# A two-block transformer kernel: another order of the new projection, the memory's norm inside the last pair of experts, and the router's token lists made first

## What is computed

```python
def moe_swiglu(h, router_w, wg, wu, wd):
    ...
    logits = (t @ router_w).astype(jnp.float32)
    top_logits, top_idx = lax.top_k(logits, TOP_K)
    top_w = jax.nn.softmax(top_logits, axis=-1)
    ...
    for e in range(N_EXPERTS):
        y = y + gates[:, e:e + 1] * swiglu(t, wg[e], wu[e], wd[e])
...
        x = x + gate2 * y
    return rmsnorm(x, final_norm_w)
...
        h = rms_norm(x, g_mix[layer])
        proj = h @ w_in[layer]
...
        log_f = jax.nn.log_sigmoid(f_logit.astype(jnp.float32)
...
        mkv = rms_norm(mem, g_mem[layer]) @ w_mem_kv[layer]
```

## Time and profile before

| | |
|---|---|
| median of 3 runs | 1531.88 us (1529.24 to 1533.62) |
| the profiled execution | 1529.77 us, span 1528.0 us |
| PE busy | 1458.8 us, 95% of the span |
| DVE busy | 1135.8 us, 74% |
| ACT busy | 769.4 us, 50% |
| experts | 610.3 to 1030 us |
| weights of the new projection first used | 1075.27 us |

### The profile page before, as it was taken

One profiled execution on the slowest core, in us unless ns is written; L12 is line 12 of the kernel. 1 busy time (PEld: TensorE's weight loads), 2 busy tenths in 40 slices (PEclk: granted clock), 3 DMA queues, 4 the chain that ended last, 5 costly groups with the idle time before them and its releaser, 6 DMA issues. The chain is left out here.

```text
span 1528.0 us, 20898 instructions
## 1 busy us (share of the span) xinstructions
PE 1458.8 (95%) x8225; PEld 1261.3 (83%) x8225; DVE 1135.8 (74%) x1245; ACT 769.4 (50%) x806; POOL 4.1 (0%) x7
## 2 busy tenths in 40 slices
PE   3998999999999997999999999999999999999999
PEld 3876799899798886878887888787787778799997
DVE  6888687876778764888988888988787677555544
ACT  1534333333463553767677677764566443443332
POOL 0000000000000000000000000000000000000000
PEclk9999999999999996999999999999999999999999
DMA  9776378877665470899998998982544335445652
GB/s 322 252 295 228 119 251 281 300 260 247 205 223 166 167 240 22 289 327 319 349 335 296 350 336 304 343 296 84 172 161 167 133 112 165 138 153 169 210 164 103
DMA packets 198424, 345.72 MB, mean 226 GB/s; under 512 B 11633, under 2 KB 90065, under 8 KB 193233
## 3 DMA queue, kind: packets, MB, share of 16 engines
q1 hardware_dynamic: 190592, 339.76, 64.5%
q10 hardware_dynamic: 7760, 4.97, 1.1%
HBM read 343.65 MB, written 1.05 MB: 226 GB/s over the span
## 5 line engine op out<-in xcount | busy, mean ns | idle before, releaser
L2000 DVE TENSOR_TENSOR wlo<-raw,whi 128x2048 fp32r<-128x2048 f32 (+2 forms) x220 | 480.0, 2192 | 163.2 <-ACT whi L637 159.4
L637 ACT ACTIVATE whi<-raw 128x2048 fp32r<-128x2048 f32 (+2 forms) x220 | 403.5, 1837 | 360.2 <-PE ps L1256 243.0
L1254 PE MATMUL ps<-whi,AH 128*128 128x512 f32 (+1 forms) x816 | 321.6, 394 | 9.0 <-DVE wlo L2000 6.0
L1256 PE MATMUL ps<-whi,AL 128*128 128x512 f32 (+1 forms) x816 | 312.2, 383 | 0.0
L1255 PE MATMUL ps<-wlo,AH 128*128 128x512 f32 (+1 forms) x816 | 312.0, 382 | 0.0
L1254 PE MATMUL ps<-AH,whi 128*128 128x256 f32 x896 | 256.3, 286 | 2.2 <-DVEq L2100 1.5
L1255 PE MATMUL ps<-AL,whi 128*128 128x256 f32 x896 | 254.8, 284 | 0.0
L1256 PE MATMUL ps<-AH,wlo 128*128 128x256 f32 x896 | 254.7, 284 | 0.0
L1254 PEld LDWEIGHTS ps<-whi,AH 128*128 128x128 f32 x816 | 153.8, 188 | 48.2 <-DVE wlo L2000 15.6
L1256 PEld LDWEIGHTS ps<-whi,AL 128*128 128x128 f32 x816 | 153.5, 188 | 28.1
L1254 PEld LDWEIGHTS ps<-AH,whi 128*128 128x128 f32 x896 | 173.3, 193 | 3.6 <-DVEq L2100 1.8
...
## 6 DMA issues: line engine op xcount, KB each, us to landing
...
```

Of the source, the lines that this page charges most:

```text
L637: act.activation(whi[:, h, 0:n], raw_at[s][:, 0:n], ACT.Copy).then_inc(w_hi, 1)
L1254: pe.matmul(o, sh, mh, start=first, stop=False)
L1256: return pe.matmul(o, sl, mh, start=False, stop=last)
L2000: dve.tensor_tensor(wlo[:, h, 0:n], raw_at[s][:, 0:n], whi[:, h, 0:n].bitcast(fp), ALU.subtract)\
```

## The change

Five things are changed:

1. A Sqrt on an idle column stands ahead of `first_squares`, so ACT loads that table there.
2. In the router DVE writes the sum of the two choices to `lg2` directly behind the choice; the constants of the lists are made earlier and the gates after the first selection. 20 fillers stand ahead of the transposes (15 before), and 4 new ones behind the token matmuls.
3. The loop over pairs has three passes, and the fourth is written out. In it ACT's queue loads the memory into `TS`, ACT squares it at j = 5 and 6, DVE makes the norm at j = 8, 11, 12 and 13 of the first expert; the two gathers are replaced by transposes of the memory (`memory_transposes`), whose features take the place of the next pair's. The gate of `Y`'s first half moves into the pass.
4. Behind the experts the memory's units follow directly. `X` is completed and normed in halves, with the final norm's scale and weight in one operation. The transposes of the new input stand inside and behind the fourth unit, followed by 3 fillers. ACT copies out the memory's products, which DVE did before.
5. The forget gate's matmul uses split operands (`three`), 24 matmuls.

```diff
-            for k0 in (0, 4):
-                m_unit(w, w_mkv, k0, 4, 0)
-            sp.wait_ge(*w.free_at[N_RAW])
-            sp.dma_start(memx, t["mem_2"][0].rearrange("(i p) n -> p i n", p=128)).then_inc(mem_in, 16)
-            for k0 in (0, 4):
-                m_unit(w, w_mkv, k0, 4, 512)
+            m_matrix(w, w_mkv, 0, 2)
...
             def first_squares(n):
 
+                act.activation(idle_col, idle_col, ACT.Sqrt)
                 act.wait_ge(x_part, 3 * n + 1)
...
+            def memory_load():
+                act.dma_start(TS[:, :, :], t["mem_2"][0].rearrange("(i p) n -> p i n", p=128)).then_inc(mem_in, 16)
+            def memory_norm(j):
+                if j in (5, 6):
+                    act.wait_ge(mem_in, 16)
+                    act.activation(flatA[:, 1024 * (j - 5):1024 * (j - 4)], TS[:, j - 5, :], ACT.Square,
+                                   accum_out=ss[:, j - 5:j - 4]).then_inc(sq_done, 1)
+                if j == 9:
+                    root(2)
+            def memory_high(bank, q):
...
+                    ins = act.activation(AH[:, kk, :], ps[:, bank + k // 2, SEQ * (k % 2):SEQ * (k % 2) + SEQ], ACT.Identity,
+                                         scale=vec[:, V_GMEM + kk:V_GMEM + kk + 1])
+                ins.then_inc(e_high, 1)
...
                         if j == 18:
+                            if last and x:
+                                next_input(1)
                             output(x, 1)
-                next_input(1)
+                if not last:
+                    next_input(1)
...
-            act.wait_ge(mem_in, 16)
-            squares(memx)
-            features_high(vec[:, V_GMEM:V_GMEM + 8])
-            his(w, 2)
-            act.wait_ge(a_ready, 2 * 6)
-            act.wait_ge(x_ready, 1)
-            squares(X)
-            act.wait_ge(x_ready, 2)
-            squares(X)
-            his(w, 2)
-            second_half(vec[:, V_GMIX:V_GMIX + 8])
+            first_unit = w.unit - LEAD
+            def memory_out(c):
+                act.wait_ge(w_used, first_unit + 2 * c + 2)
+                bank = 2 * ((PAIR_MOE + c) % 4)
+                link(act.activation(mkv[:, c], ps[:, bank:bank + 2, :], ACT.Copy))
+                act.sem_inc(ps_free, 1)
+            def half_squares(c, n):
+                for i in range(TT):
+                    act.wait_ge(x_ready, n + i * c)
+                    act.activation(flatA[:, 1024 * c + 512 * i:1024 * c + 512 * i + 512], X[:, i, 512 * c:512 * c + 512],
+                                   ACT.Square, accum_out=ss[:, 2 * c + i:2 * c + i + 1]).then_inc(sq_done, 1)
+                if c:
+                    root(2)
+            hi(w)
+            half_squares(0, 1)
+            hi(w)
+            half_squares(1, 2)
+            hi(w)
+            memory_out(0)
+            half_squares(0, 4)
+            half_squares(1, 5)
+            hi(w)
+            features_high(vec[:, V_GMIX:V_GMIX + 8], (0,))
+            memory_out(1)
+            features_high(vec[:, V_GMIX:V_GMIX + 8], (1,))
...
+            def memory_transposes(q, bank):
+                pe.wait_ge(ts_ready, 2 * stage[0] + 1 + q)
+                for k in range(4):
+                    for i in range(TT):
+                        ins = pe.transpose(ps[:, bank + k // 2, SEQ * (k % 2) + 128 * i:SEQ * (k % 2) + 128 * (i + 1)],
+                                           TS[:, i, 512 * q + 128 * k:512 * q + 128 * (k + 1)], ident)
+                ins.then_inc(e_gather, 1)
...
-                gather(w, TT, (1,))
+                if not last:
+                    gather(w, TT, (1,))
                 put_back(pair(w), 1, 1)
+                if last:
+                    pe.sem_inc(ps_free, N_EXPERTS * E_PAIRS - N_EXPERTS // 2 * E_PAIRS_2)
+                    pe.wait_ge(e_in, 2 * e + 4)
...
-            transposes(w, 15)
+            transposes(w, 20)
...
...
-                ins = pe.matmul(ps[:, bank, 16:24], ones[:, 0:128], oh[:, 0, i, :], start=i == 0, stop=i == TT - 1)
+                ins = pe.matmul(ps[:, bank, 16:24], ones[:, 0:128], lg2[:, i, :], start=i == 0, stop=i == TT - 1)
             ins.then_inc(small_mm, 1)
+            keep_busy(w, 4)
             pe.wait_ge(crowd_set, 1)
             crowd = pe.value_load(crowded[0:1, 0:1], min_val=0, max_val=1)
...
-            transposes(w, 8)
-            keep_busy(w, 4)
-            new_input()
-            m_matrix(w, 2)
-            stage[0] += 1
-            transposes(w)
-            keep_busy(w, 11)
+            stage[0] += 2
+            m_matrix(w, 1)
+            bank = pair(w)
+            m_unit(w, bank, 0, 4, KT)
+            def mixed_transposes(q):
+                pe.wait_ge(ts_ready, 2 * stage[0] - 1 + q)
+                bank = pair(w)
...
+                ins.then_inc(tp_done, 1)
+            m_unit(w, bank, 4, 4, KT, between=lambda: mixed_transposes(0))
+            mixed_transposes(1)
+            keep_busy(w, 3)
...
+                    pe.wait_ge(fox_w_set, 1)
                     for k in range(KT):
-                        ins = pe.matmul(ps[0:40, bank, 0:SEQ], wsm[:, k, 48:88], AF[:, k, :], start=k == 0, stop=k == KT - 1)
+                        ins = three(ps[0:40, bank, 0:SEQ], fox_w_high[:, k, :], fox_w_low[:, k, :], AH[:, k, :], AL[:, k, :],
+                                    k == 0, k == KT - 1)
                     ins.then_inc(small_mm, 1)
...
+            dve.tensor_scalar(upto, cst[:, C_CAUSALT:C_CAUSALT + 128], 0.0, None, ALU.is_equal)
+            dve.tensor_tensor_scan(numbers, ones[:, :], ones[:, :], 0.0, ALU.mult, ALU.add)
+            dve.memset(slot_of, 0.0)
...
+            both(dve.tensor_tensor(lg2, oh[:, 0], oh[:, 1], ALU.add), tokens_set, 1)
             dve.tensor_tensor(mm2[:, 2, :], mm2[:, 1, :], mm2[:, 0, :], ALU.subtract).then_inc(g_vec, 1)
             for i in range(TT):
                 dve.wait_ge(t_split, i + 1)
...
                 free(w, dve.tensor_tensor(t_low[:, i, :].rearrange("p (b n) -> p b n", b=2), ps[:, bank:bank + 2, :],
                                           t_high[:, i, :].bitcast(fp).rearrange("p (b n) -> p b n", b=2), ALU.subtract))
-            dve.wait_ge(g_act, 3)
-            link(dve.tensor_scalar(mm2[:, 4, :], mm2[:, 3, :], 1.0, None, ALU.add))
-            link(dve.reciprocal(mm2[:, 5, :], mm2[:, 4, :]))
...
-            dve.tensor_tensor(gates[:, :, 0:8], lgt, lg2, ALU.add)
-            dve.tensor_scalar(upto, cst[:, C_CAUSALT:C_CAUSALT + 128], 0.0, None, ALU.is_equal)
-            dve.tensor_tensor_scan(numbers, ones[:, :], ones[:, :], 0.0, ALU.mult, ALU.add)
-            dve.memset(slot_of, 0.0)
-            both(dve.tensor_tensor(oh[:, 0], oh[:, 0], oh[:, 1], ALU.add), tokens_set, 1)
             dve.wait_ge(small_mm, 3)
             bank = bank_of(w)
-            dve.tensor_tensor(slot_of[:, :, 0:8], ps[:, bank, 0:16].rearrange("p (i e) -> p i e", i=TT), oh[:, 0], ALU.mult)
+            dve.tensor_tensor(slot_of[:, :, 0:8], ps[:, bank, 0:16].rearrange("p (i e) -> p i e", i=TT), lg2, ALU.mult)
...
+            def memory_norm(j):
+                m, y, s = ms[:, 0:2], rs[:, 0:2], nt[:, 0:2]
+                if j == 8:
+                    counts["sq"] += 2
+                    dve.wait_ge(sq_done, counts["sq"])
+                    link(dve.tensor_scalar(m, ss[:, 0:2], 1.0 / D, EPS, ALU.mult, ALU.add))
+                    dve.reciprocal(y, m).then_inc(root_in, 1)
+                    counts["root"] += 1
+                if j == 11:
+                    dve.wait_ge(root_out, counts["root"])
+                    link(dve.tensor_tensor(s, y, y, ALU.mult))
+                    link(dve.tensor_tensor(s, s, m, ALU.mult))
+                    link(dve.tensor_scalar(s, s, -0.5, 1.5, ALU.mult, ALU.add))
+                    link(dve.tensor_tensor(y, y, s, ALU.mult))
+                if j in (12, 13):
+                    q = j - 12
+                    cut = slice(512 * q, 512 * q + 512)
+                    for i in range(TT):
+                        ins = dve.tensor_scalar(TS[:, i, cut], TS[:, i, cut], rs[:, i:i + 1], None, ALU.mult)
+                    ins.then_inc(ts_ready, 1)
+                    counts["ts"] += 1
+            def memory_low(bank, q):
...
+                    ins = dve.scalar_tensor_tensor(AL[:, kk, :], ps[:, bank + k // 2, SEQ * (k % 2):SEQ * (k % 2) + SEQ],
+                                                   vec[:, V_GMEM + kk:V_GMEM + kk + 1], AH[:, kk, :].bitcast(fp),
+                                                   ALU.mult, ALU.subtract)
+                ins.then_inc(e_in, 1)
+            def gated(c):
+                cut = slice(512 * c, 512 * c + 512)
+                rows_ = GB[:, 1, cut].rearrange("p (o n) -> p o n", o=1).to_broadcast([128, TT, 512])
+                link(dve.tensor_tensor(Y[:, :, cut], Y[:, :, cut], rows_, ALU.mult))
...
+                        if last and x and j == 19:
+                            gated(0)
+                            add_back(1, 1)
```

(46 more changed lines are left out.)

181 lines of the change are left out of this document (123 added, 58 removed).

## The result

| | before | changed |
|---|---|---|
| median | 1530.56 us (1525.43 to 1533.62, 4 runs) | 1506.37 us (1505.7 to 1507.2, 4 runs) |
| ratio | | 0.9838, 95% interval 0.9817 to 0.9859 |
| profiled execution | 1529.77 us, span 1528.0 us | 1505.82 us, span 1504.0 us |
| PE busy | 95% of the span | 96% |

The forecast was 1506.0. The next table puts PE's start at one place after the other beside each other. The last column says what the stretch ahead of the place gained in these two executions.

A forecast was written before the change was run, and what follows sets the result against it. PE was taken as the bound, so only its waits, fillers and half-clock time pay. 1.7 + 7.5 - 2.3 + 18.1 + 0.8 = 25.8 us, giving 1506 us against the median 1531.88; range 1499 to 1516.

The forecast's parts named there:

- Part 1: At the norms, the Sqrt table load moved ahead of the squares shortens PE's waits: gain 1.7 us, bounds 0.4 and 3.4.
- gain 1.3: At the second norm (402.94), PE's 2.02 us wait shrinks by the table load's time, 1.3 us.
- Part 2: Router: earlier token lists start the gather 5.9 us earlier, the clock gives 1.6 more: gain 7.5 us, bounds 5.0 and 11.5.
- clock term: Router's gather: only about 1 us runs at half clock, so it takes 4.3 us instead of 5.88.
- Part 3: Last pair of experts: DVE's inserted norm steps delay PE 2.6 us; cheaper transposes return 0.3: net cost 2.3 us.
- (c): Clock returns no sooner in the router and falls again ahead of the last put-back: 1509 to 1510 us, 12%.
- Part 4: Last put-back to new projection: waits, fillers and transposes fall away, start at 1057.1 instead of 1075.27: gain 18.1 us.
- The forget matmul: Forget gate: the 40-row matmul (3.65 us) becomes 24 matmuls of 256 columns, 2.9 us: gain 0.8 us.
- (a): DVE becomes the bound in the last pair and the projection behind it: 1512 to 1516 us, 15%.
- (b): The clock holds through the router: 4 us more gained, 1502 us, 12%.
- (d): Norm is ready early but PE waits for `e_in` behind DVE's queue, half the gap stays: 1515 to 1520 us, 4%.
- (e): Slower than before: ACT waits for `mem_2` ahead of its sixth unit, 1544 us at 50 us lateness; 2%.

The follow-up runs named there:

- experiment 5: The changed kernel run again, nothing altered: 1505.94 us, ratio 0.9846 to the kernel before.
- experiment 3: The changed kernel without the router's part and the early table load: 1512.39 us, ratio 0.9885 to the kernel before.
- experiment 6: The changed kernel with DVE's four small norm steps ahead of the first expert's last unit, two scalings in the second expert: 1505.5 us, ratio 0.9848.
- experiment 8: The changed kernel with the last put-back's output steps ahead of the second half of the memory's features on ACT and DVE: 1508.26 us, ratio 0.9855.
- experiment 2: The kernel before with only the router's part (lists first, 20 fillers, 4 new ones), measured twice: 1527.44 and 1529.38 us, ratio 0.9983 both times.

## Why the prediction was right

The time came out at 1506.37 against 1506.0, and the mechanism of every part is in the trace. The closeness is partly luck. The gain between the medians is 24.2 us where 25.8 were predicted, and the median of before from which the forecast was taken (1531.88) stood 1.3 above that of the four runs (1530.56). Between the two profiled executions 23.95 us were gained; without the first entry of the table, -2.95, which was not the change's (experiment 5), it would have been 26.9. Point by point:

**Part 1, 1.7 us.** Too large: 0.8 us of DVE's chain at the second norm, of which PE's wait shows 0.44 in this pair of executions, and 0.6 at the last. The step that failed is "gain 1.3": I took the load to be on the path from its start, but DVE's two small steps covered 0.47 of it, which the earlier trace rows with DVE's steps at the same time would have shown. The Trainium skill, "ScalarE: Activation LUTs", section "What ACT_TABLE_LOAD costs", adds a drain to the load; here a load was worth 0.81 us, and no row shows a drain.

**Part 2, 7.5 us.** Right in size. By time from the first filler (566.21 before, 569.18 now):

| | before | predicted | changed |
|---|---|---|---|
| transposes start | 9.49 | 8.84 | 8.70 |
| `lgt` read by DVE | 19.51 | 18.0 | 16.99 |
| gather starts | 33.11 | 27.2 | 26.18 |
| experts start | 43.74 | 36.2 | 35.13 |

The gather came 6.9 instead of 5.9 us earlier and took 3.96 instead of the predicted 4.3. The term was reckoned against a profile of before that took long at this place, though: the same instructions took 41.28 us in experiment 3. The new router took 34.96 to 36.07 in four profiles. So one pair of executions gives 5.2 us and another 8.8, and 7.5 lies between them. What holds in each is that the 5.69 us wait is gone. That the clock in the small matmuls would fall "about as long after the last filler" was right within a us if it is counted from the start of these matmuls (2.4 us before, 3.2 now), not if from the end of the fillers' row (2.2 and 3.6); over all thirteen profiles it fell 2.1 to 4.5 us behind that start. The outcome of the clock term, about 1 us of the gather at half clock, held in none of the nine profiles with new fillers: in three the gather was at full clock, in two at half for its first 2.0 and 2.6 us, and in four, behind waits of 2.7 to 2.9 us, the clock fell within it and stayed low for over 3 us.

**Part 3, 2.3 us.** The place was right: PE waits behind DVE's scaling, 1.16 us for `acc`. In sum it is 1.94 instead of 2.6 us, in four pieces, since the step took the whole 2.5 us of inserted work as late. Of these 1.94 only 0.8 hang on those steps (experiment 6). The other failed step is "ACT gets two squares (2.5 us), two table loads and the root; those waits for PE take them": the second table load, 1.28 us at 949.45, stands right ahead of ACT's part of the product, and by the trace of experiment 6 it is what makes DVE late there. The 0.3 that was to remain of the first gather came out at about 0.95 - 0.5 = 0.45 us. The wait ahead of the last put-back is 2.12 us, as rival (c) had it; the prediction put the put-back's end 1.0 us later for it, but did not see that it is free, since DVE is the bound there (experiment 8).

**Part 4, 18.1 us.** Part 3 and 4 together gave 16.8 us where 18.1 - 2.3 = 15.8 were predicted. 1.68 of the 16.8 are the stop at 1075.27, which the prediction never priced: it took the time of before as it stood, and the stop was a wait for DVE's features that the new order does away with (experiment 2). DVE's steps came in the predicted order and times: the fourth unit's `wlo` made PE wait 0.38, predicted 0.6; from the first memory unit (1027.49) to the new projection (1052.83) it took 25.3 us, predicted 22.1 + 0.6 + 1.9 + 1.3 = 25.9. "Each us that it loses goes to PE almost whole" is what experiment 8 shows: DVE comes to the gate 2.4 us later and PE to the new projection's fillers 2.4 us later (1054.14), 0.4 of each being the execution's.

**The forget matmul, 0.8.** Its 24 matmuls take 2.8 us (1063.94 to 1066.73), 2.9 predicted, against 3.6: 0.8.

**The rivals.** (a) DVE as the bound: true as a mechanism behind the put-back, but not with the price that it was given. (b) did not happen in any of ten profiles of the new router: the clock fell in the small matmuls or the transposes behind them each time. (c) is half true: in two profiles with the four fillers (the first of experiment 2, and 6) the clock came back 2.0 and 2.6 us into the gather, and the fall at the last put-back came in three of seven, for 1.1 us, not 2. Neither is in the first profile. (d) and (e) did not happen: no weight copy of ACT waits for data in the last pair, and PE is behind `e_in` for no time at all.

**How the parts add.** Alone they gave 2.8 (part 1), 3.3 and 1.9 (the router's two measurements) and 18.3 us, together 23 to 24.4 against 24.2 to 24.8. This looks like plain addition, but each of these medians is uncertain by some 2 us or more, so that the sum can't show it. The router alone loses 2 to 4 us to the stall of experiment 2, which the whole change doesn't have.
